# Hybrid DeltaNet/attention/MoE layer: work between the last two token tiles put in another order on three engines

## What is computed

```python
h = rms_norm(x, attn_norm_g);  proj = h @ w_in            # 2824 columns
# part A: 4 heads of 128: causal conv(4) + silu on q|k|v, l2-normed q and k
log_a = -exp(a_log) * softplus(alpha + dt_bias);  beta = sigmoid(b)
o_a = gated_delta_rule(q, k, v, log_a, beta)              # chunks of 64, state S carried on
y_a = rms_norm(o_a, g) * silu(z)
# part B: 8 query heads, 2 kv heads of 64, window of two chunks, learned sinks
y_b = swa_sink_attention(rms_norm(q2), rms_norm(k2), v2, sinks)
x = x + concat(y_a, y_b) @ w_out
x = x + hier_moe(rms_norm(x))                             # top 1 of 4 groups, then top 2 of 4 experts
```

## Time and profile before

| | us |
|---|---|
| median of 3 runs | 984.23 (982.5 to 984.51) |
| the profiled execution, its own time | 982.38 |
| its span, first to last instruction | 980.6 |
| around the span | 1.8 |
| PE busy | 929.4 (95%) |
| DVE busy | 593.5 (61%) |
| ACT busy | 234.7 (24%) |
| POOL busy | 216.9 (22%) |
| mean granted TensorE clock | 0.993 of 2.4 GHz |

### The profile page before, as it was taken

One profiled execution on the slowest core, in us unless ns is written; L12 is line 12 of the kernel. 1 busy time (PEld: TensorE's weight loads), 2 busy tenths in 40 slices (PEclk: granted clock), 3 DMA queues, 4 the chain that ended last, 5 costly groups with the idle time before them and its releaser, 6 DMA issues.

```text
span 980.6 us, 19083 instructions
## 1 busy us (share of the span) xinstructions
PE 929.4 (95%) x7581; PEld 682.0 (70%) x7581; DVE 593.5 (61%) x1812; ACT 234.7 (24%) x606; POOL 216.9 (22%) x302
## 2 busy tenths in 40 slices
PE   4989999999999999999999998989999999999995
PEld 4787587596686768769759675574667666777663
DVE  2356775784685687487578468788534324445443
ACT  1233231432431342234143233131001101111010
POOL 7020020020011002002002000300244454465653
PEclk9999999999999999999999999999999999999998
DMA  8920101010010110110100002811556966979621
GB/s 304 395 89 1 44 22 44 1 66 22 23 66 1 45 46 21 43 43 24 44 2 23 22 23 96 312 67 56 188 171 228 349 232 205 349 253 358 225 90 56
DMA packets 51491, 113.99 MB, mean 116 GB/s; under 512 B 11191, under 2 KB 14519, under 8 KB 51392
## 3 DMA queue, kind: packets, MB, share of 16 engines
q1 hardware_dynamic: 35072, 87.07, 24.7%
q0 software_dynamic: 14592, 25.22, 7.6%
q10 hardware_dynamic: 1728, 0.31, 0.2%
HBM read 112.54 MB, written 25.17 MB: 140 GB/s over the span
## 4 chain that ended last, share of the span: by engine, by line
PE 79%; DVE 14%; DMA 2%; issue 2%; ACT 1%; SPq 0%; POOL 0%; POOLq 0%; DVEq 0%; ACTq 0%
PE pm L417 72%; PE pm L420 6%; DVE pqkv L1398 4%; DMA w_sb<-in_w_in 2%; DVE X L1549 1%; DVE bs L1614 1%; DVE sc L1619 1%; DVE xT L1337 1%; DVE hT L1353 1%; PE pm L794 1%; DMA qkvT<-h_mid,w_sb 0%; DVE xT L1216 0%; DVE V_S L1627 0%; ACT pqkv L974 0%; DVE y_mix L1640 0%
## 5 line engine op out<-in xcount | busy, mean ns | idle before, releaser
L417 PE MATMUL pm<-hT,w_sb 128*128 128x128 f32 x1544 | 177.6, 277 | 7.3 <-DVE hT L1353 5.0
L417 PEld LDWEIGHTS pm<-hT,w_sb 128*128 128x128 f32 x1544 | 175.7, 193 | 11.9 <-DVE hT L1353 6.6
L417 PE MATMUL pm<-w_sb,hT 128*128 128x512 f32 (+1 forms) x384 | 148.0, 534 | 0.0
L1908 POOL TENSOR_TENSOR tail<-tail,rows 128x512 f32<-128x512 f32 x8 | 10.2, 1271 | 511.6 <-ACT aTm L995 511.6
L417 PE MATMUL pm<-wo_sb,pT 128*128 128x512 f32 x256 | 116.2, 603 | 4.2 <-ACT pT L1042 3.6
L417 PEld LDWEIGHTS pm<-w_sb,hT 128*128 128x128 f32 x384 | 70.8, 192 | 56.3 <-issue 52.1
L417 PE MATMUL pm<-ctmp,w_sb 128*128 128x128 f32 x768 | 88.8, 277 | 1.1 <-DVE ctmp L1696 1.1
L1398 DVE SCALAR_TENSOR_TENSOR pqkv<-ci,cw,pqkv 128x128 f32<-128x128 f32 x288 | 77.6, 343 | 19.9 <-ACT pqkv L974 19.5
L417 PEld LDWEIGHTS pm<-ctmp,w_sb 128*128 128x128 f32 x768 | 86.7, 192 | 2.6 <-issue 2.0
L417 PEld LDWEIGHTS pm<-wo_sb,pT 128*128 128x128 f32 x256 | 47.5, 193 | 56.4 <-issue 51.1
L1768 DVE TENSOR_TENSOR ci<-pm,gain 128x512 f32<-128x512 f32 x32 | 20.6, 686 | 82.7 <-PE pm L794 48.8
(11 more groups left out here) (315 smaller groups left out, 1530.5 us busy)
## 6 DMA issues: line engine op xcount, KB each, us to landing
w_sb<-in_w_gate_up SPq DMA_DIRECT2D x12, 2048.0 KB, 15.0
w_sb<-in_w_down SPq DMA_DIRECT2D x12, 1024.0 KB, 6.3
w_sb<-in_w_in SPq DMA_DIRECT2D x4, 2048.0 KB, 20.2
wo_sb<-in_w_gate_up SPq DMA_DIRECT2D x4, 2048.0 KB, 14.6
xt<-in_x SPq DMA_DIRECT2D x8, 512.0 KB, 4.6
xT<-in_x_turned SPq DMA_DIRECT2D x8, 512.0 KB, 3.5
wo_sb<-in_w_out SPq DMA_DIRECT2D x1, 4096.0 KB, 21.8
sc<-in_x SPq DMA_DIRECT2D x8, 512.0 KB, 3.5
```

The lines of the kernel that those rows point to most:

```text
L417: return pe.matmul(o_, lhsT=l_, rhs=r_, start=start, stop=stop, skip_group_check=True)
L1908: g.tensor_tensor(qk_in[:, 0:QH, :], qk_in[:, 0:QH, :], gqk[:, None, 0:DH].broadcast_to([P, QH, DH]), ALU.mult)
```

## The change

TensorE: the two decay sum products of tile 7 are issued between the two halves of the y_b output products of tile 6 (behind a wait for tile 6's `o_ready`, since they write pm[4]); in body(7) `turn_g` comes right behind the k and v transposes; the four y_a output products of the first half come behind it and ahead of the k k^T products; two of the three `keep_busy` calls go. ScalarE, in body(6) only: copy of chunk 5, then gates, then `copy_yb`, and only then `silu` and `swa_squares`. VectorE: `gate_outputs(7)` goes ahead of tile 6's output norm; `attention_norm(7)` goes behind `diff_ready` of body(7). Other tiles keep their order.

```diff
@@ tensor
+            def decay_sums(t):
+                pe.wait_ge(F.la_ready, t + 1)
+                la = fs[:, 20:20 + H]
+                mm(pm[4][:, 8:8 + H], upper[:, :], la)
+                mm(pm[4][:, 12:12 + H], ones[:, :], la).then_inc(B.sums_done, 1)
...
-                for n in range(2):
-                    out_half(t, n, range(4, KD), 4, 3)
+                out_half(t, 0, range(4, KD), 4, 3)
+                if t == NT - 2:
+                    pe.wait_ge(B.o_ready, NT - 1)
+                    decay_sums(NT - 1)
+                out_half(t, 1, range(4, KD), 4, 3)
...
-                pe.wait_ge(F.la_ready, t + 1)
-                la = fs[:, 20:20 + H]
-                mm(pm[4][:, 8:8 + H], upper[:, :], la)
-                ins = mm(pm[4][:, 12:12 + H], ones[:, :], la)
-                ins.then_inc(B.sums_done, 1)
+                if nx is not None:
+                    decay_sums(t)
+                if pv is None or nx is None:
+                    turn_g(t)
+                if nx is None:
+                    pe.wait_ge(B.yT_ready, halves_turned(pv, 1))
+                    out_half(pv, 0, range(0, 4), 4, 3)
...
-                if nx is None:
-                    keep_busy(pm[7], 1)
-                if pv is None or nx is None:
-                    turn_g(t)
-                if nx is None:
-                    keep_busy(pm[7], 1)
...
                 if nx is None:
-                    pe.wait_ge(B.yT_ready, halves_turned(pv, 1))
-                    out_half(pv, 0, range(0, 4), 4, 3)
                     out_half(pv, 1, range(0, 2), 4, 3)
@@ scalar
-                if nx is not None:
+                if t == NT - 2:
+                    ahead(5)
                     gates(nx)
-                ahead(5)
+                    copy_yb(t)
+                else:
+                    if nx is not None:
+                        gates(nx)
+                    ahead(5)
...
                     swa_squares(nx)
-                    if t == NT - 2:
-                        copy_yb(t)
                     z_tanh(nx)
@@ vector
                 v.tensor_scalar(dT[:, :, :], dT[:, :, :], 0.0, None, ALU.min).then_inc(B.diff_ready, 1)
+                if not nx:
+                    last_front[0].attention_norm()
...
+                if t == NT - 2:
+                    nx.gate_outputs()
                 v.wait_ge(B.sq_ready, 2 * t + 2)
...
                     nx.silu()
-                    nx.gate_outputs()
                     if t == NT - 2:
-                        nx.attention_norm()
                         last_front.append(nx)
                     else:
+                        nx.gate_outputs()
```

## The result

The changed kernel takes 979.09 us (median of 5 runs, 976.38 to 980.72) against 984.31 us (5 runs, 982.5 to 985.5): ratio 0.9945 with a 95% interval of 0.9926 to 0.9964, 5.2 us less, between 3.5 and 7.3. I had forecast 980.8 and a range from 979.2: the direction was right, and the time fell just under the range. Its profiled execution took 977.75 us, with a span of 975.9, 4.7 us under the span of before.

The account below looks back on a forecast made before the run. Bound: a chain 79% on TensorE, 14% on VectorE. Decay differences start 4.4 us earlier (including gap 1.45, clock 1.6); attention_norm costs 0.75, collisions 0.25: 3.4 off 982.38 gives 979.0, 980.8 on the median's scale; range 979.2 to 983.3.

Parts of the forecast that it names:

- the border: Passage from tile 6 to tile 7, up to the start of tile 7's inverse: forecast 3.4 us earlier.
- the 1.6 us of the half clock: Output products behind TensorE's 2.87 us gap: a gap of 1.4 us most likely keeps full clock, saving 1.6 us.
- my own sign of a wrong prediction: Clock under 1.00 anywhere from 610 to 650 us was one of the stated signs that the prediction is wrong.
- the stall: Tile 6's output norm on VectorE: GpSimd multiplications hold its first small instruction 0.7 us, or 1.15 if not slipping in.
- The beta copy: VectorE's copies of the decay sums: one may be held by a GpSimd instruction until 620.15, still in time for turn_g.
- TensorE idle ahead of the inverse: Before tile 7's inverse: TensorE done at 628.6, VectorE at 629.6, so TensorE waits 1.0 us.
- the drain: ScalarE table switches: the skill adds about 1380 ns each, 2.8 us later for two; the prediction followed the trace instead.
- the rule on the shared port pair: VectorE and GpSimd: every small instruction meeting a GpSimd one costs up to that one's rest.
- Rival B: Output products at the border: the clock falls all the same, 1.6 us return; gain 2.7, 981.5 us; chance 0.13.
- Rival C: Border: VectorE and GpSimd collide more, a late copy holds turn_g by 0.5 us; gain 2.2, 982.0 us; chance 0.12.
- Rival D: Tile 7's inverse: without two keep_busy calls the clock falls, three losses of 1.6 us, 4.9 total; 985.7 us; chance 0.06.
- Rival E: Gain given back later, or a moved wait longer than reckoned, VectorE's norm 3.4 us later; 984.2 us; chance 0.12.

Follow-up runs that it names:

- e1: Kernel before with only tile 0's turn_g moved ahead of the k k^T products; ratio 0.9977 (0.9953 to 1.0).
- r2_after: The changed kernel unaltered, timed a third time; ratio 0.9961 (0.9947 to 0.9975) against the kernel before.
- r_after: The changed kernel unaltered, timed again; ratio 0.9968 (0.9954 to 0.9982) against the kernel before.
- r3_after: The changed kernel unaltered, profiled once more; span 978.0 us.
- e2: The changed kernel with tile 0 put back in its old order; ratio 0.9978 (0.9956 to 1.0) against the kernel before.
- e3: Kernel before with ScalarE's part of the change alone; ratio 0.9979 (0.9961 to 0.9998).
- e5: The changed kernel with the two removed keep_busy calls put back behind the k k^T products; ratio 0.9948, 978.32 us against 983.78 for the kernel before.
- e6: The changed kernel with VectorE's attention_norm in the wait for turn_g and the beta copy behind it; ratio 0.9926 (0.9908 to 0.9944) against the kernel before.
- e6b: The same kernel as e6, timed again beside a repeat of e7; ratio 0.9945, median 979.6 us against 983.78 for the kernel before.
- e7: e6 plus gates in two parts, window row copy between Ln and Tanh, attention squares summed during the turn_g wait; ratio 0.9947 against the kernel before.
- b1: Kernel before, unchanged, profiled a second time; span 980.0 us.
- b2: Kernel before, unchanged, profiled a third time; span 980.9 us.
- e4: The changed kernel without ScalarE's part, so the window row copy comes behind silu and squares again; profiled span 982.3 us.
- e8: Kernel before with TensorE's order in body(7) alone, two keep_busy calls gone, sums not amid the y_b products; profiled span 978.2 us.

## Why the prediction was right or wrong

**The step that failed is the list of what the change moves.** I costed the border alone and wrote that the other tiles keep their order. e1 and the marks A show 1.04 us at tile 0, which stay. The border came to 3.23 us against 3.4 forecast. Added, the marks give 4.3 us, 980.0 on the scale of the median; with tile 0 in the sum, my range would have begun a microsecond lower and held the result. But 980.0 lies inside the range as it was stated, too: that the measured 979.09 lies under it takes the 0.9 us of the next paragraph as well.

**The rest of the 5.2 us.** Over the 4.3 us of the marks, 0.9 us remain, inside the interval of 3.5 to 7.3. The two later timed comparisons gave 3.2 and 3.8 us. What makes executions of one kernel differ is seen in the last column of the table: near 57, 107, 631, 680 and 711 us the clock falls in some executions and not in others. In mark C a fall costs 1.66 us; at 107 the stretch from tile 0 to chunk 5 is 532.34 to 532.39 us with it and 530.60 to 530.69 without, in kernels that share A = 11.76, so 1.7 us. The mean clock of the timed executions says the same: the five of the changed kernel took 976.38 us at 0.996, 977.75 at 0.995, 979.09 and 979.19 at 0.993, and 980.72 at 0.991. In the comparison of r2_after, five executions of each kernel had 0.993; their means are 982.24 and 979.43, 2.8 us apart; in the comparison of r_after both kernels had 0.983 in the mean and lie 3.4 us apart. The marks give 2.7 us without the 1.6 us of the half clock. So by the marks the change is worth 2.7 us of work and 1.6 us of one fall less, and much of what differs between the comparisons goes with how many other falls an execution has.

Whether the change alters how often these others come is open. Near 107 the clock fell in six of the seven profiles with A = 12.80 and in five of the eleven with A = 11.76, which would favour the change. Near 631 it fell in two of the four profiles of the changed kernel and in none of the kernel before, which speaks against it. In those four profiles it fell near 106 or near 630 and never at both, so the two are not independent. No run tried to steer any of this, and 18 profiles are too few to tell it from chance.

**Point by point at the border**, with 1.51 us added to the times after:

- ScalarE: copy_yb at 609.50, forecast 609.50. First output product 610.13, forecast 610.15.
- Clock: no fall at the output products behind the 1.39 us gap, in none of the nine profiles that have it (after, r_after, r2, r3, e2, e3, e5, e6, e6b). The 1.6 us were right. But a clock under 1.00 somewhere from 610 to 650 was my own sign of a wrong prediction: there was none in after and r_after, and one near 630 in r2_after and r3_after.
- Sums amid the products: at 613.66, forecast 613.7. y_a transposes at 617.54, forecast 617.7.
- gate_outputs: first instruction at 609.62 and 0.17 long, forecast 609.60 and 0.17. It waited 1.00 us for the Tanh.
- GpSimd: the stall moved to L1209 and L1210, 0.91 + 0.38, which is 0.7 and 0.2 over their own 0.2. silu ended at 618.96, forecast 618.9.
- The beta copy was held 1.09 us and turn_g not, as said.
- dT at 620.58 against 620.45; L1514 held 0.3 longer than alone; L1537 ended at 629.85 against 629.6; copy at 630.64 against 630.5.
- TensorE idle ahead of the inverse: 1.57 against 1.0. It was done at 628.34, forecast 628.6, and VectorE was 0.25 late; together that is 0.5 of the difference of 0.57.

**Table loads and the shared port.** The table loads take 1.28 us and the next activation starts 0.01 to 0.02 us later, in e7 too (608.19 to 609.48); by the drain that the Trainium skill (ScalarE: Activation LUTs, "What ACT_TABLE_LOAD costs") adds, estimated at 2.8 us for the two switches, the first product could not have started at 610.13. The measurement decides. The prediction applied the rule on the shared port pair to every small instruction. That is wider than the rule: the Trainium skill (SBUF — State Buffer, "SBUF: two separate sides") states the lock for VectorE instructions in a 2-port mode or with two SBUF inputs. The traces agree with the narrower form as far as they go. In each kernel a small instruction with all inputs in SBUF waits out the rest of a GpSimd one, while the copies from pm (L1507 and L1508, 0.15 us) and e6's reduction with its one SBUF input (L1387, 0.81 us) ran beside a GpSimd multiplication and were not held. Which of the held ones with one input were in such a mode no trace shows.

**The rivals.** Rival B (the clock falls at the output products all the same) didn't happen. Rival C (more collisions) happened only in its small part. Rival D, the fall ahead of the inverse after keep_busy was taken out, is half right: the clock falls there in three of the five profiles with the 1.57 us gap (r2_after, r3_after, e2), and e5 with the calls put back has neither gap nor fall. But it comes back after 1.66 us of cost, not after three such losses, and never made the kernel slower than before. Rival E, the gain given back later, didn't happen by a wait: from the copy that ends mark B to the end of the span both kernels need 346.7 to 346.8 us in the profiles of before, after, b1, b2 and b3. By the clock a part is given back in some executions: 1.66 us at the new gap, in r2_after and r3_after.

## What to carry to other kernels

Read every condition of a moved line for the iterations it covers; a line moved for the last tile moved here for the first as well, and the shared branch was worth a quarter of the gain. When a chain is shortened on one engine, look up what the next engine does in the new slack: here VectorE became the bound, and a reduction of 0.8 us that had been free cost time until it was put into the wait for turn_g. Compare profiles by marks around the change instead of by spans: with no fall of the clock inside they repeated to 0.02 us, and to 0.3 with one, where whole executions spread over 4. Compare whole executions at the same mean granted clock, where they allow it.

## What the runs showed of the hardware that I had not expected

- The clock of TensorE falls behind gaps of 1.33 us (e4, near 634) to 1.57 us in some executions and not in others of the same kernel, while it never fell behind the 0.93 us gap of e6 and e7 or behind the 1.39 us one at 608. Behind the 2.87 us gap it fell in all seven profiles that have it.
- How long it stays down behind the same 2.87 us gap differs: 16 products take 8.6 to 8.8 us in the kernel before and in e1, 10.21 in e8 and 10.43 in e4.
- A small VectorE instruction, 0.17 us alone, that meets a GpSimd multiplication of 128x512 takes 0.9 to 1.2 us: L1204 of before (1.14), L1209 (0.91), the copy of beta (1.09), L1217 of e7 (1.12), L1367 of before (1.23). A reduction from SBUF put in that place was not held: 0.81 us in e6, as alone.
